# Differential attention of a two-block kernel: value product feature by feature in three fp32r passes, norm by a product with ones

## The chip, the cores and the metric

The program runs on one core of one Trainium2 chip. Its metric is the device time of one execution in microseconds, as a median over runs. Everything is float32 in and out, batch 1, 512 tokens, width 1024.

## The reference, cut to what matters

Two blocks follow each other. The first (pooling mixer, sparse attention, feed-forward) is not touched. The second has two layers; each projects the normed input, runs three branches (gated linear attention "a", sparse attention "b", differential attention "c"), gates them, merges them and adds the result. The change is in branch c of both layers:

```
def _diff(q, k, v, ..., lambda_init):          # 4 heads of 2 x 64, values of 128
    q, k = _rms(q, qn_g), _rms(k, kn_g)
    p = softmax(where(allowed, q k^T * 64**-0.5, -inf))      # two maps per head, 512 x 512
    attn = p[:, :, 0] - lam * p[:, :, 1]
    out = attn @ v                                           # [512 tokens, 4 heads, 128]
    out = out * rsqrt(mean(out**2, over 128) + 1e-6) * (1 - lambda_init)

y_c = _diff(...) * silu(cz)                     # then y_c @ w_br[2], gated and merged
```

`allowed` is causal by chunks of 64, so of the 4 x 4 blocks of 128 x 128 per map only the 10 on and below the diagonal are computed.

## The kernel before, in words

**Number format.** Most products are made of float32 operands split into a high part (rounded to fp32r, written "r" here) and a low part (the rest). A product is then three matmuls, high x high, low x high, high x low (helper `three`, L286 to L291, and `high_first`, L293 to L304, which puts the products with the low part of the weights last so that it can arrive late). A matmul on unsplit float32 tiles is one instruction that the profile shows as two records.

**Weights.** They come as a stream of chunks of 128 x 2048 through two slots. SyncE loads a chunk, ScalarE makes its high part (`act_conv`, L278), VectorE (`dve_conv`, L283) or GpSimd its low part. Every section of the layer ("cz", "cgate", "gv", "gq", "cbr" and so on) has a fixed order of tiles; TensorE puts a tile in one of two PSUM banks `pp` and waits, through the semaphore `evac`, until the tile two before has been copied out (`pe_tile`, L309). The sections "in the wide form" (`pe_wide`) have tokens on the partitions of the result; `pe_tile_part` gives features on the partitions.

**Order.** Each engine's program of a layer is written out by hand (`pe_layer`, `act_layer`, `dve_layer`, `pool_layer`, L1421 to L2160); engines meet at semaphores only, and each engine runs strictly in its order. Attention steps are laced between projection pieces, so that TensorE has matmuls while ScalarE and VectorE do the softmax.

**Branch c, a head.** In step s (0 to 4, each with quarters i = 0 to 3) TensorE computes head s's scores in the banks `ps` and `pt` (`pe_score_diff`, L1337), VectorE the row maxima, ScalarE the exponentials and their sums (`act_exp_diff`, L1353), VectorE combines the two maps (`dve_combine`, L1363): p1 = p1 + c * p2, unnormalised, with c = -lam * sum1 / sum2. It also keeps 1 / sum1 (`r1`, L1378). In step s+1 the blocks are turned by TensorE transposes (`pe_turn_attn`, L1243) and copied back by ScalarE over the attention tile (`act_turned_attn`, L1258). `pe_pv_tm` (L1265) then multiplies: the turned attention block is the stationary operand, 128 value columns move, in plain float32, 10 blocks per head; the output has tokens on partitions. VectorE scales it by r1 (`dve_o_diff`, L2087), GpSimd squares it and multiplies it by the gate `z_c` (L2139, L2141), VectorE sums the squares (`dve_o_sum`), ScalarE takes one square root for all, VectorE inverts it (`inverse_root`) and scales four tiles (L1997). In the middle of section "gq" TensorE turns these four tiles (16 transposes, L1209), ScalarE and VectorE split them into high and low parts (L1220, L1224), and section "cbr" multiplies them by the branch weights.

**Order on VectorE in a step s = 1 or 2**: at i = 2 the maxima of row block 3, `dve_combine` of row block 2, the low part of a turned key (L1224), the low part of a weight chunk (L283); at i = 3 `dve_combine` of row block 3. In step 3 there is no key to turn. TensorE multiplies the value blocks 2 and 3 of the head before at i = 0 of the step after that, ahead of the scores of its head.

**Order on ScalarE at the end**: a weight chunk, the sigmoid of the first half of the gates (`xT`, L1752), section "gq" tile 0 copied out, four high parts, "gq" tile 1 copied out (L1758), a weight chunk (L278), the sigmoid of the second half (`work`, L1763), two exponentials and a small one for branch a (L1766, L1767), then the tiles of "cbr" copied out (L1046).

Of the kernel before, what the change touches and what calls it, by code (L numbers as in the profile page):

```python
# [107 lines left out]
WIDE = ("gki", "bq", "bk", "bv", "cq", "ck", "cv", "cz", "gv", "gz")  # L108
KI = 344
KI_IK, KI_ALR, KI_IW = 256, 320, 336  # L110
FOUR_BANKS = ("q", "gki", "bq", "bk", "bv", "cz")
# [17 lines left out]
def two_block_kernel(nc, x_in, pos_in, w_in, vec_in, cst_in, msk_in, cmpw_in, small_in, out):  # L129
    with ExitStack() as ctx:  # L130
# [7 lines left out]
        xT = sb("xT", [P, KT, S], F32)  # L138
        hhi, hlo = sb("hhi", [P, KT, S], F32R), sb("hlo", [P, KT, S], F32R)
# [15 lines left out]
        alr_f = sb("alr_f", [P, S], F32)  # L155
        p_odd = sb("p_odd", [P, EVEN], F32)
# [62 lines left out]
        o_out, ring_in, v_in = sem("o_out"), sem("ring_in"), sem("v_in")  # L219
        cs_ready, cs_sub, cs_exp, cs_p = sem("cs_ready"), sem("cs_sub"), sem("cs_exp"), sem("cs_p")  # L220
# [26 lines left out]
        ix_acc, x_kept = sem("ix_acc"), sem("x_kept")  # L247
        o_turned, o_sq, o_sum, o_gated = sem("o_turned"), sem("o_sq"), sem("o_sum"), sem("o_gated")
# [446 lines left out]
        vr = [[rv(9216 + 1024 * b + 512 * y, 4, P) for y in range(2)] for b in range(2)]  # L695
        yr = [rv(0, 4, S), rv(2048, 4, S)]
# [16 lines left out]
        o_tm, osq_f = xT[:, 4:8, :], wv(14848, S)  # L713
# [5 lines left out]
        gq_f, kd_f, za_f, la_f = wv(6144, 2, S), wv(7168, 4, 256), wv(8192, 4, 256), wv(9216, 4, 256)  # L719
# [6 lines left out]
        r1 = [nst[:, 232 + 4 * b:236 + 4 * b] for b in range(2)]  # L726
# [17 lines left out]

        def turned_attn(s, kb):

            p = attn(s)[:, P * kb + STEP * kb:]
            return bass.AP(p.tensor, p.offset, [p.ap[0], [STEP, QT - kb], [1, P]])

        def low_no(v):  # L750

            l = (v - U1) // 8
            return 4 * (U1 + 4 * l + v - U1 - 8 * l)
# [489 lines left out]
        def pe_turn_attn(pe, l, v, s, kbs):  # L1243

            if kbs[0] == 0:
# [2127 lines left out]
```

## Time and profile before

| | us |
|---|---|
| median of 3 runs (1859.45 to 1859.85) | 1859.71 |
| the profiled execution's own time | 1859.72 |
| its span, first to last instruction | 1857.8 |
| TensorE matmuls busy | 1853.4 |
| weight loads of TensorE | 1537.6 |
| VectorE | 1239.6 |
| ScalarE | 899.4 |
| GpSimd | 397.6 |

The granted TensorE clock is 1.000 over the whole span, that is 2.4 GHz. A busy time is the union of the instructions' durations; matmuls are pipelined, so the distance from one start to the next (the start column of the timeline) is what a matmul costs, and its duration is longer.

### The profile page before, as it was taken

How to read it: one execution, taken by the hardware profiler on the slowest of the kernel's cores; microseconds unless marked ns; L12 is line 12 of the kernel's file. 1: busy time of each engine (PE TensorE's matmuls, PEld its weight loads, DVE VectorE, ACT ScalarE, POOL GpSimd, SP SyncE). 2: the span in 40 equal slices, each digit the busy share in tenths (PEclk: the TensorE clock that was granted, in tenths of full speed). 3: DMA queues.
4: the chain of work that ended last, by engine and by line, in shares of the span. 5: the costliest groups of instructions: out<-in, count | busy, mean ns of one | idle time of the engine just before them, and what ended most of it. 6: DMA issues, size and time to landing. Idle time of an engine off the chain costs nothing.

```text
span 1857.8 us, 25108 instructions
## 1 busy us (share of the span) xinstructions
PE 1853.4 (100%) x9597; PEld 1537.6 (83%) x9597; DVE 1239.6 (67%) x2022; ACT 899.4 (48%) x1417; POOL 397.6 (21%) x211
## 2 busy tenths in 40 slices
PE   9999999999999999999999999999999999999999
PEld 7977778788898988788888888888888888888887
DVE  7888657684783876688656755465689665666553
ACT  6564565544443455534455554444543445646442
POOL 1020012240440530245010000131235101010211
PEclk9999999999999999999999999999999999999999
DMA  6211113222232243222122123224122222112321
GB/s 243 97 69 69 46 68 139 94 99 100 91 114 91 91 145 127 91 91 91 69 91 94 46 91 114 108 97 159 69 91 91 79 81 91 71 69 91 137 91 68
DMA packets 26894, 178.98 MB, mean 96 GB/s; under 512 B 3232, under 2 KB 4128, under 8 KB 6560
## 3 DMA queue, kind: packets, MB, share of 16 engines
q1 hardware_dynamic: 24768, 163.97, 24.4%
q10 hardware_dynamic: 2016, 13.51, 1.9%
q8 instruction: 73, 1.20, 0.3%
q14 instruction: 37, 0.30, 0.0%
HBM read 171.18 MB, written 6.29 MB: 96 GB/s over the span
## 4 chain that ended last, share of the span: by engine, by line
PE 99%; DVE 0%; DMA 0%; ACT 0%; DVEq 0%; issue 0%; ACTq 0%
PE pp L299 34%; PE pp L303 17%; PE pp L289 9%; PE pp L291 9%; PE pp L290 9%; PE po L299 4%; PE po L303 2%; PE po L979 1%; PE po L1269 1%; PE pt L950 1%; PE po L291 1%; PE po L290 1%; PE po L289 1%; PE ps L1347 1%; PE po L1209 1%; PE ps L856 1%
## 5 line engine op out<-in xcount | busy, mean ns | idle before, releaser
L283 DVE TENSOR_TENSOR wlo<-wraw,whi 128x2048 fp32r<-128x2048 f32 x116 | 271.4, 2340 | 186.6 <-ACT whi L278 186.0
L278 ACT ACTIVATE whi<-wraw 128x2048 fp32r<-128x2048 f32 x143 | 273.2, 1910 | 63.3 <-PE pp L303 63.3
L299 PE MATMUL pp<-hhi,whi 128*128 128x512 f32 x639 | 259.0, 405 | 0.0
L299 PE MATMUL pp<-hlo,whi 128*128 128x512 f32 x639 | 249.7, 391 | 0.0
L299 PE MATMUL pp<-whi,hhi 128*128 128x512 f32 (+2 forms) x528 | 206.3, 393 | 0.0
L299 PE MATMUL pp<-whi,hlo 128*128 128x512 f32 (+2 forms) x528 | 199.9, 380 | 0.0
L303 PE MATMUL pp<-hhi,wlo 128*128 128x512 f32 x639 | 173.9, 390 | 0.0
L2114 POOL TENSOR_TENSOR wlo<-wraw,whi 128x2048 fp32r<-128x2048 f32 x26 | 120.4, 4632 | 248.7 <-ACT whi L278 248.7
L289 PE MATMUL pp<-split,whi 128*128 128x512 f32 x402 | 156.8, 390 | 0.0
L291 PE MATMUL pp<-split,wlo 128*128 128x512 f32 x402 | 156.4, 389 | 0.0
L290 PE MATMUL pp<-split,whi 128*128 128x512 f32 x402 | 156.4, 389 | 0.0
L299 PEld LDWEIGHTS pp<-hhi,whi 128*128 128x128 f32 x639 | 120.0, 188 | 33.8 <-issue 8.9
L303 PE MATMUL pp<-wlo,hhi 128*128 128x512 f32 (+2 forms) x528 | 144.0, 380 | 0.0
L303 PEld LDWEIGHTS pp<-hhi,wlo 128*128 128x128 f32 x639 | 119.9, 188 | 25.8
L299 PEld LDWEIGHTS pp<-hlo,whi 128*128 128x128 f32 x639 | 120.2, 188 | 22.3 <-issue 0.5
L289 PE MATMUL pp<-hhi,whi 128*128 128x512 f32 x303 | 118.9, 392 | 0.0
L291 PE MATMUL pp<-hhi,wlo 128*128 128x512 f32 x303 | 117.9, 389 | 0.0
L290 PE MATMUL pp<-hlo,whi 128*128 128x512 f32 x303 | 117.9, 389 | 0.0
L299 PEld LDWEIGHTS pp<-whi,hhi 128*128 128x128 f32 x528 | 99.3, 188 | 17.7 <-issue 1.9
L303 PEld LDWEIGHTS pp<-wlo,hhi 128*128 128x128 f32 x528 | 97.0, 188 | 18.8
L299 PEld LDWEIGHTS pp<-whi,hlo 128*128 128x128 f32 x528 | 99.4, 188 | 15.4
L299 PE MATMUL pp<-split,whi 128*128 128x512 f32 x444 | 107.2, 390 | 0.0
(544 smaller groups left out, 3703.9 us busy)
## 6 DMA issues: line engine op xcount, KB each, us to landing
wraw<-weights SPq DMA_DIRECT2D x150, 1024.0 KB, 4.8
out_t<-xT ACTq DMA_DIRECT2D x4, 1024.0 KB, 4.1
xT<-out_t ACTq DMA_DIRECT2D x2, 2048.0 KB, 8.8
work<-cmp_w ACTq DMA_DIRECT2D x1, 2048.0 KB, 8.7
xT<-x_t ACTq DMA_DIRECT2D x1, 2048.0 KB, 7.5
wraw<-weights SPq DMA_DIRECT2D x7, 256.0 KB, 7.8
xT<-x_t SPq DMA_DIRECT2D x3, 512.0 KB, 8.4
out_t<-xT SPq DMA_DIRECT2D x3, 512.0 KB, 2.6
```

Source lines behind the costliest of these rows:

```text
L278: nc.scalar.activation(whi[:, slot, :], wraw[:, slot, :], ACT.Copy).then_inc(w_hi, 1)
L283: nc.vector.tensor_tensor(wlo[:, slot, :], wraw[:, slot, :], whi[:, slot, :].bitcast(F32), ALU.subtract).then_inc(w_lo, 1)
L289: nc.tensor.matmul(out_ap, ah, bh, start=start, stop=False)
L290: nc.tensor.matmul(out_ap, ah, bl, start=False, stop=False)
L291: return nc.tensor.matmul(out_ap, al, bh, start=False, stop=stop)
L299: nc.tensor.matmul(out_ap, *pair, start=(start and n == 0 and part == 0), stop=False)
L303: last = nc.tensor.matmul(out_ap, *pair, start=False, stop=(stop and n == len(steps) - 1))
L856: last = nc.tensor.matmul(front_bank(s, i, g)[:, at:at + w], qr[t % 2][x][rows, i * P:i * P + P], kr[b][y][rows, 0:w], start=(x + y == 0 a ...
L950: last = nc.tensor.transpose(pt[g][:, at:at + P], p_buf(s, g)[:, STEP * i + kb * P:STEP * i + kb * P + P], ident)
L979: last = nc.tensor.matmul(po[g][y_rows(g), kb * P:S].rearrange("p (i m) -> p i m", m=P), v32[:, kb, at:at + 64], turned(s, g, kb), start=( ...
L1209: last = nc.tensor.transpose(bank[:, i * P:i * P + P], src[:, i * P:i * P + P], ident)
L2114: nc.gpsimd.tensor_tensor(wlo[:, c % 2, :], wraw[:, c % 2, :], whi[:, c % 2, :].bitcast(F32), ALU.subtract).then_inc(w_lo, 1)
```

## The change

It replaces, in both layers:

- section "cz" (the gate) from the wide form to `pe_tile_part`, features on partitions; weights are laid out accordingly; it no longer uses the banks `po`
- `pe_pv_tm` by `pe_pv_diff`: the values, split by GpSimd into two parts, are stationary; the turned attention moves, 512, 384, 256 and 128 columns wide, in three passes; ScalarE's copy of the turned blocks rounds to fp32r, and VectorE makes their low part (`dve_turned_attn`); the waits of `pe_turn_attn`, `pe_score_diff` and the value product are on VectorE's `pt_lo` instead of ScalarE's `pt_hi`
- `dve_combine`: both maps are normalised there (one more pass over the row block), `r1` goes
- the result of the value product is squared and copied out by ScalarE (`act_o_diff`); GpSimd multiplies, squares and makes the low part of the square; TensorE sums squares over the features with a matrix of ones, two passes per head, in section "gv"; ScalarE takes the inverse root of a full 128 x 512 tile per head; VectorE corrects it (`dve_o_norm`); no transposes follow
- on ScalarE, the sigmoid of `xT` moves from before section "gq" to behind it

```
-WIDE = (..., "cv", "cz", "gv", "gz")
+WIDE = (..., "cv", "gv", "gz")
-FOUR_BANKS = ("q", "gki", "bq", "bk", "bv", "cz")
+FOUR_BANKS = ("q", "gki", "bq", "bk", "bv")

 def pe_turn_attn(...):
-                pe.wait_ge(pt_hi, 4 * v)
+                pe.wait_ge(pt_lo, 4 * v)
...
-                pe.wait_ge(pt_hi, 4 * v + kbs[0] - 1)
+                pe.wait_ge(pt_lo, 4 * v + kbs[0] - 1)
-        def pe_pv_tm(pe, v, s, kb, bank):
-            pe.wait_ge(pt_hi, 4 * v + kb + 1)
-            for i in range(kb, QT):
-                last = nc.tensor.matmul(bank[:, i * P:i * P + P], attn(s)[:, STEP * i + kb * P:STEP * i + kb * P + P],
-                                        c_f[:, kb, s * P:s * P + P], start=(kb == 0 and i == 0), stop=(kb == QT - 1))
+        def dve_turned_attn(dve, v, s, kbs):
+            for kb in kbs:
+                dve.wait_ge(pt_hi, 4 * v + kbs[-1] + 1)
+                nc.vector.tensor_tensor(turned_low(s, kb), turn_bank(kbs, kb).rearrange("p (i m) -> p i m", m=P),
+                                        turned_attn(s, kb).bitcast(F32), ALU.subtract).then_inc(pt_lo, 1)
+        def pe_pv_diff(pe, l, v, s, kb, bank):
+            if kb == 0:
+                pe.wait_ge(diff_v, 4 * l + s + 1)
+            pe.wait_ge(pt_lo, 4 * v + kb + 1)
+            last = three(bank[:, kb * P:S].rearrange("p (i m) -> p i m", m=P), [y[:, kb, :] for y in diff_parts[s % 2]],
+                         (turned_attn(s, kb), turned_low(s, kb)), kb == 0, kb == QT - 1)
 def pe_score_diff(...):
             if i == 2 and s >= 2:
-                pe.wait_ge(pt_hi, 4 * (U1 + 8 * l + 4 + s - 1))
+                pe.wait_ge(pt_lo, 4 * (U1 + 8 * l + 4 + s - 1))
 def dve_combine(...):
-            nc.vector.reciprocal(c[:, 0:1], sums[:, 2 * i + 1:2 * i + 2])
+            nc.vector.reciprocal(c, psum_[s % 2][:, 2 * i:2 * i + 2])
             dve.drain()
-            nc.vector.scalar_tensor_tensor(out=c[:, 1:2], in0=c[:, 0:1], scalar=nlam[:, l:l + 1],
-                                           in1=sums[:, 2 * i:2 * i + 1], op0=ALU.mult, op1=ALU.mult)
+            nc.vector.tensor_scalar(c[:, 1:2], c[:, 1:2], nlam[:, l:l + 1], None, ALU.mult)
+            nc.vector.tensor_scalar(p1, p1, c[:, 0:1], None, ALU.mult)
...
-                nc.vector.reciprocal(r1[s % 2], sums.rearrange("p (i g) -> p i g", g=2)[:, :, 0])
 def pe_layer(pe, l):
...
             for p in range(4, 8):
                 pe_wide(pe, "gv", l, p)
-            pe_tile_part(pe, "gq", l, 0, 0, 1)
-            for x in range(4):
-                pe.wait_ge(y_scaled, 8 * l + x + 1)
-                pe_t(pe, D_BANKS[x], o_tm[:, x, :])
-            pe_tile_part(pe, "gq", l, 1, 0, 1)
+                for x in {4: range(3), 5: range(3, 4)}.get(p, ()):
+                    pe.wait_ge(o_turned, 4 * l + (3 if x < 3 else 4))
+                    pe.wait_ge(o_sq, 8 * l + x + 1)
+                    nc.tensor.matmul(norm_banks[x][:, :], ones_r[:, :], square_hi[x], start=True, stop=False)
+                    nc.tensor.matmul(norm_banks[x][:, :], ones_r[:, :], square_lo[:, x, :], start=False, stop=True).then_inc(t_done, 1)
+            for n in range(2):
+                pe_tile_part(pe, "gq", l, n, 0, 1)
 ScalarE:
+        def act_o_diff(act, l, s):
+            act.wait_ge(pv_done, U1 + 8 * l + 4 + s + 1)
+            nc.scalar.activation(square_hi[s], po[s % 2][:, :], ACT.Square)
+            nc.scalar.activation(o_fm[:, s, :], po[s % 2][:, :], ACT.Copy).then_inc(o_turned, 1)
 def act_layer(act, l):
...
+            for x in range(4):
+                act.wait_ge(t_done, tb + 8 + x + 1)
+                nc.scalar.activation(o_fm[:, x, :], norm_banks[x][:, :], ACT.Abs_reciprocal_sqrt, scale=1.0 / P,
+                                     bias=con(C_EPS)).then_inc(o_root, 1)
...
-            nc.scalar.activation(xT[:, 0:4, :], xT[:, 0:4, :], ACT.Sigmoid)
+            for x in range(4):
+                act.wait_ge(o_norm, 4 * l + x + 1)
+                nc.scalar.activation(yr[0][:, x, :], z_c[:, x, :], ACT.Copy, scale=con(C_1ML + l)).then_inc(t_hi, 1)
...
             act_next(act, "gq", l, c0, slot0)
+            nc.scalar.activation(xT[:, 0:4, :], xT[:, 0:4, :], ACT.Sigmoid)
             nc.scalar.activation(wv(4096, 4 * S), wv(4096, 4 * S), ACT.Sigmoid).then_inc(gates_in, 1)
 VectorE:
+        def dve_o_norm(dve, l, x):
+            y, t, z = o_fm[:, x, :], norm_t[x % 2], z_c[:, x, :]
+            dve.wait_ge(o_root, 4 * l + x + 1)
+            nc.vector.scalar_tensor_tensor(out=t, in0=y, scalar=-0.5 / P, in1=y, op0=ALU.mult, op1=ALU.mult)
+            nc.vector.scalar_tensor_tensor(out=t, in0=norm_banks[x][:, :], scalar=EPS * P, in1=t, op0=ALU.add, op1=ALU.mult)
+            dve.wait_ge(o_gated, 8 * l + x + 1)
+            nc.vector.scalar_tensor_tensor(out=z, in0=t, scalar=1.5, in1=z, op0=ALU.add, op1=ALU.mult).then_inc(o_norm, 1)
 GpSimd:
+            def diff_values_in(s):
+                if s >= 2:
+                    pool.wait_ge(pv_done, v0 + 4 + s - 1)
+                split_pool(pool, diff_parts[s % 2], c_f[:, :, s * P:s * P + P]).then_inc(diff_v, 1)
...
+                nc.gpsimd.tensor_tensor(z, z, o, ALU.mult)
+                nc.gpsimd.tensor_tensor(o, o, o, ALU.mult)
+                nc.gpsimd.tensor_tensor(square_lo[:, s, :], o, square_hi[s].bitcast(F32), ALU.subtract).then_inc(o_sq, 1)
```

## Rows read from the trace of the kernel before

**Rows 1.** The page: busy times, and the chain that ended last

```profile
PE 1853.4 (100%) x9597; PEld 1537.6 (83%) x9597; DVE 1239.6 (67%) x2022; ACT 899.4 (48%) x1417; POOL 397.6 (21%) x211
...
PE 99%; DVE 0%; DMA 0%; ACT 0%; DVEq 0%; issue 0%; ACTq 0%
```

**Rows 2.** Timeline of TensorE, branch c: start, duration, what, count

```profile
1032.85 1.05 PE L1269 MATMUL po<-work 128*128 128x128 f32 x8
1033.74 0.49 PE L1254 MATMUL pt<-cst,work 128*128 128x128 f32 x3
...
1039.62 0.83 PE L1269 MATMUL po<-work 128*128 128x128 f32 x6
...
1074.56 0.83 PE L1269 MATMUL po<-work 128*128 128x128 f32 x6
```

**Rows 3.** Timeline of TensorE, value products of branch b in three passes

```profile
899.01 0.33 PE L289 MATMUL po<-split 128*128 128x384 f32 x1
...
899.53 0.38 PE L1233 MATMUL pt<-cst,work 128*128 128x128 f32 x2
...
903.61 0.28 PE L289 MATMUL po<-split 128*128 128x256 f32 x1
...
903.96 0.27 PE L1233 MATMUL pt<-cst,work 128*128 128x128 f32 x1
...
907.22 0.28 PE L290 MATMUL po<-split 128*128 128x128 f32 x1
907.34 0.27 PE L291 MATMUL po<-split 128*128 128x128 f32 x1
```

**Rows 4.** Timeline of TensorE, section "cbr", product of 512 columns

```profile
1121.16 0.39 PE L289 MATMUL pp<-split,whi 128*128 128x512 f32 x1
...
1121.84 0.39 PE L289 MATMUL pp<-split,whi 128*128 128x512 f32 x1
```

**Rows 5.** Timeline of TensorE, the turns within section "gq"

```profile
1106.43 1.03 PE L1209 MATMUL po<-cst,xT 128*128 128x128 f32 x8
...
1108.09 0.48 PE L299 MATMUL pp<-hhi,whi 128*128 128x512 f32 x1
```

**Rows 6.** Timeline of VectorE, branch c, steps 1 and 3

```profile
1035.43 0.75 DVE L1224 SCALAR_TENSOR_TENSOR split<-po,vec,split 128x512 fp32r<-128x512 f32 x1 [1.28 <-ACT split L1220]
1036.10 2.28 DVE L283 TENSOR_TENSOR wlo<-wraw,whi 128x2048 fp32r<-128x2048 f32 x1
...
1039.49 0.17 DVE L1378 RECIPROCAL nst<-nst 128x4 f32<-128x4 f32 x1
...
1072.80 0.17 DVE L1378 RECIPROCAL nst<-nst 128x4 f32<-128x4 f32 x1
```

**Rows 7.** Timeline of ScalarE, branch c, step 1

```profile
1038.44 0.55 ACT L1262 ACTIVATE work<-pt 128x256 f32<-128x256 f32 x2 [3.04 <-PE pt L1254]
```

**Rows 8.** Groups by form, VectorE: count, then busy us, mean ns, idle

```profile
L1388 DVE TENSOR_SCALAR work<-work,stat 128x512 f32<-128x512 f32 x8 | 3.9, 486 | 0.6
...
L1000 DVE TENSOR_TENSOR split<-pt,split 128x256 fp32r<-128x256 f32 x8 | 3.4, 424 | 10.1 <-ACT split L994 10.1
```

**Rows 9.** Timeline of ScalarE, sections "gq" and "cbr"

```profile
1106.69 1.92 ACT L1752 ACTIVATE xT<-xT 128x2048 f32<-128x2048 f32 x1
...
1113.84 0.60 ACT L1758 ACTIVATE work<-pp 128x512 f32<-128x512 f32 x1 [2.45 <-PE pp L303]
...
1118.07 1.28 ACT L1766 ACT_TABLE_LOAD   x1
...
1120.63 0.60 ACT L1046 ACTIVATE work<-pp 128x512 f32<-128x512 f32 x1
```

**Rows 10.** Timeline of GpSimd, branch c, step 2

```profile
1045.97 1.28 POOL L2141 TENSOR_TENSOR xT<-xT,work 128x512 f32<-128x512 f32 x1
```

**Rows 11.** Timeline of VectorE, the same moment

```profile
1046.10 1.30 DVE L1374 SCALAR_TENSOR_TENSOR work<-work,nst 128x128 f32<-128x128 f32 x1
...
1047.84 0.48 DVE L1374 SCALAR_TENSOR_TENSOR work<-work,nst 128x256 f32<-128x256 f32 x1
```

More of the change, by code:

```diff
@@ L695, in two_block_kernel @@
         vr = [[rv(9216 + 1024 * b + 512 * y, 4, P) for y in range(2)] for b in range(2)]
+        diff_low = [rv(TRI * b, TRI) for b in range(2)]
+        diff_parts = [[rv(2560 + 1024 * b + 512 * y, 4, P) for y in range(2)] for b in range(2)]
         yr = [rv(0, 4, S), rv(2048, 4, S)]
@@ L712, in two_block_kernel @@
         z_b, cq_tm, ck_tm, z_c = xT[:, 0:4, :], xT[:, 4:8, :], wv(4096, 4, S), wv(6144, 4, S)
-        o_tm, osq_f = xT[:, 4:8, :], wv(14848, S)
+        o_fm = xT[:, 4:8, :]
+        square_hi = [rv(4608, S), rv(9984, S), rv(10496, S), work_r[:, 14848:15360]]
+        square_lo = xT_r[:, 4:8, :]
+        norm_banks = (po[0], ps[0], ps[1], po[1])
+        norm_t = [split_f[:, 7168 + 512 * b:7680 + 512 * b] for b in range(2)]
         p2_f = [wv(14592, P), wv(13568, 256), wv(14080, 384), wv(13568, S)]
@@ L1485, in pe_layer @@
             pe.wait_ge(y_ready, 4 * l + 4)
-            for p in range(6):
-                pe_wide(pe, "cz", l, p)
+            for n in range(3):
+                pe_tile_part(pe, "cz", l, n, 0, 1)
             tb, v0 = tb + 8, v0 + 4
@@ L1492, in pe_layer @@
             pe_t(pe, ps[1], ck_tm[:, 0, :])
-            for p in range(6, 8):
-                pe_wide(pe, "cz", l, p)
+            pe_tile_part(pe, "cz", l, 3, 0, 1)
             for s in range(4 + 1):
@@ L1507, in pe_layer @@
                     for kb in diff_values(s, i) if s >= 1 and i > 0 else ():
[L1508 to L1509 removed]
                         if kb == 0 and s == 4:
                             pe.wait_ge(o_turned, 4 * l + 2)
[L1512 removed]
+                        pe_pv_diff(pe, l, v0 + s - 1, s - 1, kb, po[(s - 1) % 2])
                     if s >= 1 and diff_turns(s, i):
@@ L1693, in act_layer, with gate_tile @@
                 sq_c(4 + tt), ck_tm[:, tt, :], ACT.Square).then_inc(ln_sq, 1))
-            act.wait_ge(ln_sum, 4 * l + 2)
+            act.wait_ge(ln_sum, 3 * l + 2)
             nc.scalar.activation(ln_root, ln_ss, ACT.Sqrt, scale=1.0 / 64, bias=con(C_EPS)).then_inc(ln_rt, 1)
-            act_after_first(act, "cz", l)
-            for i in range(2):
-                act_wide(act, "cz", l, i, z_c[:, i, :], ACT.Silu)
+            cz, _, tz, _ = section("cz", l)
+            pz, sz = par_of("cz", l)
+            def gate_tile(n):
+                act.wait_ge(mm_done, tz + n + 1)
+                nc.scalar.activation(z_c[:, n, :], pp[(pz + n) % 2][:, :], ACT.Silu).then_inc(evac, 1)
+            for n in range(2):
+                gate_tile(n)
+            act_next(act, "cz", l, cz, sz)
             tb, v0 = tb + 8, v0 + 4
@@ L1702, in act_layer @@
             act_t(act, tb + 1, kr[0][0], ps[1], col(V_CK + l))
-            for i in range(2, 4):
-                act_wide(act, "cz", l, i, z_c[:, i, :], ACT.Silu)
+            for n in range(2, 4):
+                gate_tile(n)
             act.dma_start(wa2_f[:, :], small_in[:, 6 * P + 256 * l:6 * P + 256 * l + 256]).then_inc(wa2_in, 16)
@@ L1712, in act_layer @@
                             act.wait_ge(tr_done, 4 * (v0 + s - 2) + 4)
+                        if i == 0 and s >= 2:
+                            act_o_diff(act, l, s - 2)
                         for rows in by_bank(diff_rows(s, i)):
@@ L1858, in dve_layer @@
             par0, _ = par_of("iq", l)
+            if l == 0:
+                nc.vector.tensor_copy(ones_r[:, :], ones)
             c0 = section("gki", l)[0]
@@ L2012, in dve_layer, with y_low @@
                                            op1=ALU.subtract).then_inc(la_split, 1)
+            def y_low(x):
+                dve.wait_ge(t_hi, tb + 8 + x + 1)
+                nc.vector.scalar_tensor_tensor(out=yr[1][:, x, :], in0=z_c[:, x, :], scalar=con(C_1ML + l),
+                                               in1=yr[0][:, x, :].bitcast(F32), op0=ALU.mult,
+                                               op1=ALU.subtract).then_inc(t_lo, 1)
+            y_low(0)
             dve_conv(dve, c0 + 3, (slot0 + 1) % 2)
-            for x in range(4):
-                dve_t(dve, tb + 8 + x, [y[:, x, :] for y in yr], D_BANKS[x], con(C_1ML + l))
+            for x in range(1, 4):
+                y_low(x)
             dve_next(dve, "gq", l)
             dve.wait_ge(decayed, l + 1)
+            dve.drain()
             for i in range(QT):
@@ L3260, in _stream @@
         columns(br[1], 512)
-        rows(w[:, 5720:6232])
+        columns(w[:, 5720:6232])
         columns(gate[:, 2048:3072])
```

111 lines of the change are left out of this document (50 added, 61 removed).

## The prediction

> **What bounds the kernel now.** Three views, in this order. First the busy times and the chain that ended last: TensorE is busy in 1853.4 of 1857.8 us and the chain is 99% TensorE [rows 1]. So the time is the sum of what TensorE issues plus whatever it waits for; work saved on VectorE, ScalarE or GpSimd is worth nothing unless TensorE would have waited for it, and work added there costs nothing until it makes TensorE wait. Second the timeline of TensorE through branch c, to price matmuls by the distance between starts, since durations overlap. Third the timelines of the other engines at the places where TensorE meets a semaphore, to see how long before TensorE's arrival each is fulfilled. I found no wait of TensorE in branch c in either layer; layer 1 repeats layer 0, so all sums are per layer and then doubled. They are made against the profiled execution's own 1859.72 us (span 1857.8), which is 0.01 from the median.
>
> **A. What TensorE issues.** The value product before: an instruction of 128 moving columns is two records, and eight records take 1032.85 to 1033.74, 0.11 us a record [rows 2]. Per head 20 records: 2.22 us. After: three passes over 512, 384, 256 and 128 columns. 512 columns: 0.68 for three (1121.16 to 1121.84) [rows 4]. 384: 0.52, 256: 0.35, and 128: 0.12 a pass, so 0.35 [rows 3]; a pass of 128 columns costs no less than one of 256. Sum 1.90, so 0.32 saved per head and 1.3 per layer. Little, because the narrow blocks pay three passes for what two records did.
>
> The turns behind: 16 transposes take 1106.43 to 1108.09, 1.66 us [rows 5]; in their place 8 products with ones over 512 columns, 8 x 0.227 = 1.81 [rows 4]. About +0.1. Section "cz" has 96 matmuls of 512 columns in either form: nothing. Its four banks become two, so tile 2 needs tile 0 copied out, but a tile lasts 24 x 0.227 = 5.4 us and the copy 0.6; that work hides it. The transposes of the attention blocks stay. A = -1.2 per layer, between -0.8 and -1.6.
>
> **B. The wait for the low parts.** TensorE takes blocks 2 and 3 of head 0 at 1039.62 [rows 2]. Before, it needed ScalarE's copies alone, done at 1038.44 + 0.55 = 1038.99 [rows 7]: 0.6 to spare. Now it needs VectorE's subtraction, which stands in VectorE's order behind the low part of a key, the low part of a weight chunk (2.28) and the combination of row block 3. That chain is set by ScalarE's copy of the turned key (the wait shown at 1035.43) and runs without a pause to 1039.49, where the combination is over [rows 6]. So VectorE can't begin before about 1039.5, even if nothing were added. Added: the normalising pass over 512 columns, 0.49 less its overlap with the small instruction ahead of it, and r1 gone: +0.3. Then the subtraction of 256 columns, 0.42 [rows 8]. The key's turn itself comes 0.2 earlier, as block 0's product is 0.2 shorter. Ready: 1039.49 - 0.2 + 0.3 + 0.42 + 0.05 for the signal = 1040.1. TensorE arrives 0.35 earlier than before (blocks 0 and 1), at 1039.3. It waits 0.8. Block 3 (0.3 later) is ready in time, as block 2 takes 0.35.
>
> For head 1 the same pattern stands 17.88 us on. All of it hangs on events of TensorE in the same step, so the wait comes back rather than being absorbed by the first. ScalarE has there two more passes over a PSUM bank (square and copy) ahead of the exponentials, GpSimd five operations instead of two; I add 0.2: 1.0. For head 2 (TensorE at 1074.56 [rows 2]) VectorE is done at 1072.80 [rows 6], early, because no key is turned in that step. But block 1's subtraction now stands ahead of the chunk: +0.6 (nearest row: 0.42 for 256 columns [rows 8]), the two longer combinations +0.6, and its own wait for ScalarE's copy of block 1 some 0.3; then 0.42 for block 2. 1072.80 + 0.6 + 0.6 + 0.3 + 0.42 = 1074.7 against 1074.2: 0.4 to 0.5, taken as 0.4. Head 3 has the blocks one by one with 1.4 us of other matmuls between a turn and its product: nothing.
>
> B = 0.8 + 1.0 + 0.4 = 2.2 per layer. From below: if the passes overlap better and head 2 makes it, 1.0. From above: one GpSimd operation of 1.28 in the way in each of three steps, 2.2 + 2.3 = 4.5.
>
> Why such an operation can be in the way: a VectorE pass over 128 columns that began at 1046.10, while GpSimd's operation of 1045.97 to 1047.25 ran, took 1.30, against 0.48 for 256 columns just after it [rows 10, 11]. By the Trainium skill ("SBUF — State Buffer", section "SBUF: two separate sides") VectorE, when it reads two SBUF inputs, and GpSimd share one port pair as an exclusive lock held for the whole instruction. The trace agrees: the pass ended just after GpSimd's did. It speaks against this change, which gives GpSimd more; it is the rival "lock" below.
>
> **C. The sigmoid that moved.** ScalarE's order in the tail decides when "cbr" tile 0 is copied out, and TensorE needs this before tile 2, as `pp` has two banks. Before: copied at 1120.63 + 0.60 = 1121.23 [rows 9]; TensorE began tile 2 at 1121.84 [rows 4]. 0.6 to spare. ScalarE went from "gq" tile 1 at 1113.84, which TensorE sets, without a pause to that copy. The sigmoid of `xT` stood before all this at 1106.69, followed by a stretch in which ScalarE waited 2.45 for TensorE [rows 9]: it was free. Now it stands inside the chain: 1.92. Its table load comes with it, since the logarithm's table is in use until then: 1.28, as the one at 1118.07 [rows 9]. The copy comes at 1124.4, TensorE waits 3.2 - 0.6 = 2.6. Nothing else on TensorE lies between to soak it up: the distance from the end of "gq" to "cbr" tile 2 is unchanged. C = 2.6 per layer. From below 0, if the load or the order differ from what I read; from above 3.2, if the spare 0.6 is taken by something else.
>
> By the Trainium skill ("ScalarE: Activation LUTs", "What ACT_TABLE_LOAD costs") a switch costs about 2.66 us with its drain. The rows at 1118.07 show 1.28 and the next instruction directly behind; with the page's figure C would be 4.0, an estimate from that page, and the total 2.8 higher. I go by the row.
>
> **D. The tail of the norm.** Inverse root of four full tiles on ScalarE (4 x 0.6 and a load of 1.28), four GpSimd products, twelve VectorE passes of about 0.7 instead of four. From TensorE's last product with ones to "cbr" there are two pieces of "gv" and two tiles of "gq", 24 + 48 matmuls of 0.227, 16 us, and 2.7 more for branch a's products. VectorE's new chain, laid out in order: norm 8.5, chunk 2.3, the wait for the logarithm, branch a's 4.7, the first low part 0.7, chunk 2.3, three low parts 2.0; it ends about 1.5 to 3 before TensorE needs each. D = 0, above 2 per layer with the lock.
>
> **Sum.** A + B + C + D = -1.2 + 2.2 + 2.6 + 0 = +3.6 per layer, +7.2 for two: 1866.9.
>
> **Rivals.** About 0.2%, 3.7 us, is what a measurement of this kernel can tell from no change.
>
> 1. One of the two waits does not come. Without B: -2.4 + 5.2 = +2.8, 1862.5. Without C: -2.4 + 4.4 = +2.0, 1861.7. For: B is a difference of 0.8 between chains 5 us long, and C rests on one table load and 0.6 us of slack. Against: both chains run without a pause in the rows. Chance 0.21.
>
> 2. Not slower: TensorE's arithmetic alone decides, since both waits are hidden. Place: the value product; price -1.2 per layer; 1859.7 - 2.4 = 1857.3. It decides if VectorE's low parts are ready by 1039.3 and the copy of "cbr" tile 0 by 1121.8. For: before the change TensorE never waited in this stretch. Against: rows 6, where VectorE is busy past 1039.3 even without the additions. Chance 0.08; it is within 0.2%, as 2.4 is below 3.7.
>
> 3. The lock: GpSimd's extra operations (about 3.5 us more per head, and four products beside VectorE's norm) hold VectorE up. A delay of 1.28 in two of three steps and 1 in D: +3.6 per layer above some of my B, say +2 per layer net. 1866.9 + 4 = 1870.9. For: rows 10 and 11. Against: at the critical ends of the steps GpSimd has long finished; its work falls where VectorE has slack, and subtractions that read PSUM take only one SBUF input. Chance 0.18.
>
> **How the numbers follow.** Forecast 0.53, rival 1 0.21, rival 2 0.08, rival 3 0.18. The forecast's own range is 1863.5 to 1869.5 from the bounds of A and B. The whole: from rival 1's 1861.5 to 1872, which leaves out rival 2, some of rival 1's tail and the worst of the lock. Slower by over 0.2% (above 1863.4): forecast, lock and a little of rival 1, 0.71. Within 0.2%: most of rival 1 and of rival 2, 0.25. Faster: 0.04.
>
> **What would show it.** Value products on "po" in three passes, 1.9 us a head, and no plain float32 matmul there: A. TensorE idle before the 256-column product in three steps of a layer, released by VectorE's subtraction: B; if it is released by GpSimd (values) or ScalarE, B has the wrong cause. TensorE idle of 2 to 3 us inside "cbr" before its third tile, released by ScalarE's copy, with the sigmoid of `xT` and a table load right before: C. If the table load stays ahead of "gq", C is 1.3. TensorE idle before "cbr" tile 0 would mean D. VectorE passes of over 1 us for 128 to 512 columns at those places mean the lock. The forecast is wrong if TensorE shows no idle time in branch c.

## The result, and the profile after the change

The changed kernel takes 1869.99 us (median of 6 executions, 1868.11 to 1870.25), the kernel before it 1859.76 in the same comparison (1859.45 to 1860.46): ratio 1.0052, 95% interval 1.0041 to 1.0062. That is 10.2 us slower; forecast were 7.1 more (1866.9, whole range 1861.5 to 1872.0; the forecast's own range ended at 1869.5). The profiled execution took 1870.24 with a span of 1868.5, and all working below is made against it. The six times fall into two groups, four from 1869.9 to 1870.25 with a mean granted clock of 0.999 and two near 1868.15 with 1.000; experiment 5 says what lies between them.

The page of the changed kernel, busy times and the chain that ended last (beside [rows 1]):

```profile
PE 1855.7 (99%) x9517; PEld 1533.2 (82%) x9517; DVE 1264.6 (68%) x2071; ACT 912.4 (49%) x1439; POOL 443.9 (24%) x243
...
PE 95%; ACT 1%; DVE 1%; DVEq 1%; DMA 0%; issue 0%; ACTq 0%; SPq 0%
```

TensorE issues 80 matmuls fewer and is no longer 99% of the chain: VectorE and ScalarE have entered it. Who they are stands in the waits of TensorE (what waited and on whom: total us, times, longest):

```profile
PE po L294 <- DVE split L1286: 4.1, 6, 1.1
PE pp L294 <- ACT work L1059: 4.1, 2, 2.2
PE pt L2375 <- DVE work L2866: 1.2, 1, 1.2
```

The third row is in the kernel before as well, outside the layers. The first is the value product waiting for VectorE's low part, three times per layer; the second is "cbr" waiting for ScalarE's copy, once per layer. Both are new. To see why the first comes, VectorE in step 1 of layer 0 (start, duration, what), which answers to [rows 6]:

```profile
1035.64 0.75 DVE L1237 SCALAR_TENSOR_TENSOR split<-po,vec,split 128x512 fp32r<-128x512 f32 x1
1036.31 2.28 DVE L288 TENSOR_TENSOR wlo<-wraw,whi 128x2048 fp32r<-128x2048 f32 x1
1038.51 0.16 DVE L1393 RECIPROCAL nst<-nst 128x2 f32<-128x2 f32 x1
1038.75 0.21 DVE L1395 TENSOR_SCALAR nst<-nst,stat 128x1 f32<-128x1 f32 x1
1038.88 0.48 DVE L1396 TENSOR_SCALAR work<-work,nst 128x512 f32<-128x512 f32 x1
1039.43 0.75 DVE L1398 SCALAR_TENSOR_TENSOR work<-work,nst 128x512 f32<-128x512 f32 x1
1040.10 0.62 DVE L1286 TENSOR_TENSOR split<-pt,work_r 128x256 fp32r<-128x256 f32 x2
```

and TensorE at the same moment, beside its product at 1039.62 in [rows 2]:

```profile
1040.67 0.36 PE L294 MATMUL po<-work_r,split 128*128 128x256 f32 x1 [0.80 <-DVE split L1286]
1040.86 0.28 PE L295 MATMUL po<-split 128*128 128x256 f32 x1
```

VectorE runs without a pause from the low part of the key to the subtraction, which begins at 1040.10; TensorE could have begun 0.80 us earlier than it did. For the second wait, ScalarE from the copy of "gq" tile 1 to that of "cbr" tile 0, beside [rows 9]:

```profile
1115.60 0.60 ACT L1791 ACTIVATE work<-pp 128x512 f32<-128x512 f32 x1 [2.88 <-PE pp L308]
1116.09 1.91 ACT L283 ACTIVATE whi<-wraw 128x2048 fp32r<-128x2048 f32 x1
1118.02 1.28 ACT L1793 ACT_TABLE_LOAD   x1
1119.31 1.92 ACT L1793 ACTIVATE xT<-xT 128x2048 f32<-128x2048 f32 x1
1121.13 1.90 ACT L1794 ACTIVATE work<-work 128x2048 f32<-128x2048 f32 x1
1123.05 1.28 ACT L1797 ACT_TABLE_LOAD   x1
1124.35 1.09 ACT L1797 ACTIVATE work<-pt 128x512 f32<-128x512 f32 x2
1125.32 0.19 ACT L1798 ACTIVATE work<-po 128x16 f32<-128x16 f32 x1
1125.61 1.09 ACT L1059 ACTIVATE work<-pp 128x512 f32<-128x512 f32 x2
```

and TensorE there. Matmuls before the wait start 0.23 us apart, as in [rows 4]; behind it, 0.43 apart for a while:

```profile
1123.43 0.39 PE L295 MATMUL pp<-split,whi 128*128 128x512 f32 x1
1123.66 0.39 PE L296 MATMUL pp<-split,wlo 128*128 128x512 f32 x1
1126.26 0.75 PE L294 MATMUL pp<-split,whi 128*128 128x512 f32 x1 [2.22 <-ACT work L1059]
1126.81 0.63 PE L295 MATMUL pp<-split,whi 128*128 128x512 f32 x1
1127.24 0.63 PE L296 MATMUL pp<-split,wlo 128*128 128x512 f32 x1
```

Two windows of equal length side by side (length, busy time of the engines, then the granted clock as the third number from the end):

```profile
1126.34:1129.76 3.42, 3.42 (x8) 2.69 (x9) 3.27 (x7) 0.36 (x1) 0.00 (x0) 0.50 0.00 0
1129.76:1133.18 3.42, 3.42 (x16) 2.80 (x15) 1.67 (x3) 0.60 (x1) 0.00 (x0) 1.00 0.00 0
```

8 matmuls where 16 fit: for 3.42 us the granted clock was half of full speed (1.2 instead of 2.4 GHz), so half of 3.42, 1.7 us, is lost.

Laying the starts of TensorE's matmuls in the two traces side by side, and taking the waits from start to start (so with the overlap of two matmuls, 0.17 us, that a wait takes away), the difference of 10.7 us between the spans of the two profiled executions comes out so:

| part | forecast, both layers | layer 0 | layer 1 | sum |
|---|---|---|---|---|
| A, TensorE's own instructions | -2.4 | -0.96 | -1.01 | -1.97 |
| B, waits for low parts of blocks 2 and 3 | +4.4 | 0.97 + 0.97 + 0.47 | 1.32 + 0.97 + 0.47 | +5.17 |
| C, wait for the copy of "cbr" tile 0 | +5.2 | 2.38 | 2.02 | +4.40 |
| D, tail of the norm | 0 | 0.29 | 0.65 | +0.94 |
| half clock behind C | not forecast | 1.7 | 0 | +1.7 |
| start of the program, before the change | not forecast | | | +0.42 |

The sum is 10.66. Row A is the remainder; it includes 0.11 us per layer that the first matmul behind C's wait loses, so up to that point it is -1.07 and -1.12. C and D belong together: D is spent just ahead of C's wait and shortens it, and C + D is 2.67 in both layers. The last row is no part of the change: within the first 15 us of the program the profiles of this case drift apart by up to 0.9 us (against the kernel before, -0.27 in experiment 2 and +0.64 in experiment 4).

### The profile page after: what moved, and what is told of

Its sections match the earlier page's. It is cut to its first block, busy times and chain, and to the rows that moved or that the text cites. A ratio compares the mean times of both kernels' runs of the same rounds, so it can differ in the third digit from the quotient of the medians.

```text
span 1868.5 us, 25085 instructions
## 1 busy us (share of the span) xinstructions
PE 1855.7 (99%) x9517; PEld 1533.2 (82%) x9517; DVE 1264.6 (68%) x2071; ACT 912.4 (49%) x1439; POOL 443.9 (24%) x243
## 4 chain that ended last, share of the span: by engine, by line
PE 95%; ACT 1%; DVE 1%; DVEq 1%; DMA 0%; issue 0%; ACTq 0%; SPq 0%
PE pp L304 33%; PE pp L308 16%; PE pp L294 9%; PE pp L296 9%; PE pp L295 9%; PE po L304 3%; PE po L308 2%; PE po L294 1%; PE po L296 1%; PE po L295 1%; PE po L992 1%; PE pt L963 1%; PE ps L1372 1%; PE ps L869 1%; DVEq L1394 1%; PE ps L295 1%
## 5 line engine op out<-in xcount | busy, mean ns | idle before, releaser
L304 PE MATMUL pp<-hhi,whi 128*128 128x512 f32 x703 | 283.9, 404 | 0.0
L304 PE MATMUL pp<-hlo,whi 128*128 128x512 f32 x703 | 274.7, 391 | 0.0
L304 PE MATMUL pp<-whi,hhi 128*128 128x512 f32 (+2 forms) x496 | 193.6, 392 | 0.0
L308 PE MATMUL pp<-hhi,wlo 128*128 128x512 f32 x703 | 189.8, 390 | 0.0
L304 PE MATMUL pp<-whi,hlo 128*128 128x512 f32 (+2 forms) x496 | 187.4, 380 | 0.0
L304 PEld LDWEIGHTS pp<-hhi,whi 128*128 128x128 f32 x703 | 132.0, 188 | 36.3 <-issue 8.9
L308 PEld LDWEIGHTS pp<-hhi,wlo 128*128 128x128 f32 x703 | 131.9, 188 | 28.5
L304 PEld LDWEIGHTS pp<-hlo,whi 128*128 128x128 f32 x703 | 132.3, 188 | 24.8 <-issue 0.5
L308 PE MATMUL pp<-wlo,hhi 128*128 128x512 f32 (+2 forms) x496 | 135.4, 379 | 0.0
L294 PE MATMUL pp<-hhi,whi 128*128 128x512 f32 x303 | 118.9, 392 | 0.0
L296 PE MATMUL pp<-hhi,wlo 128*128 128x512 f32 x303 | 117.9, 389 | 0.0
L295 PE MATMUL pp<-hlo,whi 128*128 128x512 f32 x303 | 117.9, 389 | 0.0
L1028 POOL CAST split<-work 128x512 fp32r<-128x512 f32 x22 | 14.6, 666 | 383.4 <-PE po L296 204.6
```

The source lines that it names most:

```text
L294: nc.tensor.matmul(out_ap, ah, bh, start=start, stop=False)
L295: nc.tensor.matmul(out_ap, ah, bl, start=False, stop=False)
L296: return nc.tensor.matmul(out_ap, al, bh, start=False, stop=stop)
L304: nc.tensor.matmul(out_ap, *pair, start=(start and n == 0 and part == 0), stop=False)
L308: last = nc.tensor.matmul(out_ap, *pair, start=False, stop=(stop and n == len(steps) - 1))
```

## Experiments

My theory: four terms as in the forecast, B set by VectorE's queue (the chunk's low part ahead of the passes), C by ScalarE's order, the half clock by TensorE's standing still, D by VectorE and GpSimd holding each other up. The kernels are the changed kernel with one thing altered, unless said otherwise; the kernel before, beside them, took 1859.85 to 1859.98 (1859.76 beside the changed kernel), so a difference between two experiments is known to about 0.2 us.

**1. The sigmoid back where it was** (e1_sigmoid_back).

```
+            nc.scalar.activation(xT[:, 0:4, :], xT[:, 0:4, :], ACT.Sigmoid)   # ahead of y's high parts
...
-            nc.scalar.activation(xT[:, 0:4, :], xT[:, 0:4, :], ACT.Sigmoid)   # behind the copies of "gq"
```

> The changed kernel with the sigmoid of xT put back ahead of the high parts of y, where it stood before the change. My theory: TensorE's idle time of 2.2 and 1.9 us within cbr (waiting for ScalarE's copy of tile 0) goes in both layers, and with it the stretch of 3.4 us at half clock behind the first of them. 1870.0 - 4.4 - 1.7 = 1863.9 us. The high parts of y come 3.2 us later but VectorE does not reach their low parts before 1114.7, so nothing is added. Rival: the copy is late for another reason (the low parts of y, GpSimd's lock on VectorE's passes); then most of the idle time stays and the time is above 1868.

Measured 1864.01 (1863.67 to 1864.1), ratio 1.0022 [1.0012, 1.0031], clock 1.00 in all 11 executions. Of the new waits this one is left:

```profile
PE po L294 <- DVE split L1286: 4.1, 6, 1.1
```

The wait at "cbr" is gone, and 5.98 us with it, for the 4.40 of C and the 1.7 of the half clock, 6.1. C is shown, cause and size.

**2. The chunk's low part moved behind the value product** (e2_chunk_after): in steps 1 to 3 VectorE makes the low part of the "cgate" chunk at the end of quarter 3 instead of quarter 2.

```
-                    if 1 <= s <= 3 and i == 2 or s == 4 and i == 0:
+                    if 1 <= s <= 3 and i == 3 or s == 4 and i == 0:
```

> The changed kernel with VectorE's low part of the weight chunk of cgate moved, in steps 1 to 3, from the end of quarter 2 to the end of quarter 3, behind the combination of row block 3 and the low parts of turned blocks 2 and 3. My theory: the wait of TensorE for these low parts (0.97, 0.97 and 0.47 us a layer, start to start) comes from the place in VectorE's queue; the low parts are then ready at about 1039.7 against 1039.5, so 4.8 of 5.2 us go: 1865.2 us. Rival: the added passes alone or GpSimd's operations make them late; then the wait stays above half a us in each step and the time above 1867.

Measured 1867.77 (1866.67 to 1868.73), ratio 1.004 [1.0026, 1.0054]: a miss, half of the gain. Its waits of TensorE:

```profile
PE pp L294 <- ACT work L1059: 4.0, 2, 2.2
...
PE pp L308 <- DVE wlo L288: 0.9, 2, 0.5
PE pt L1267 <- issue: 0.5, 2, 0.2
```

The row of the value products is gone, so the chunk's place is a cause of B (the added pass is the other, experiment 6). But 2.29 us of VectorE's time don't vanish: the low part of the "gv" chunk is late now (0.65 per layer from start to start), and two turns (0.30 and 0.40), as I read it since the maxima and with them the exponentials are late; the row of the turns names no releaser. 1.35 of the 2.41 in layer 0 are given back.

**3. The sigmoid in ScalarE's gap** (e3_sigmoid_gap): between the copies of "gq" tile 0 and tile 1, where ScalarE waits for TensorE anyway.

```
                 nc.scalar.activation(gq_f[:, n, :], pp[(par0 + n) % 2][:, :], ACT.Copy, scale=0.125).then_inc(evac, 1)
+                if n == 0:
+                    nc.scalar.activation(xT[:, 0:4, :], xT[:, 0:4, :], ACT.Sigmoid)
...
-            nc.scalar.activation(xT[:, 0:4, :], xT[:, 0:4, :], ACT.Sigmoid)   # behind the copies of "gq"
```

> The changed kernel with the sigmoid of xT between the copies of gq tile 0 and gq tile 1, where ScalarE waits 2.9 us for TensorE. My theory: 3.2 us of sigmoid and table load nearly fit there, gq tile 1 is copied 0.25 us later, and the copy of cbr tile 0 is in time: as e1, 1863.9 us (up to 0.4 more). Rival: as for e1, above 1868.

Measured 1863.78 (1863.57 to 1864.15), ratio 1.0021 [1.0012, 1.003]. As experiment 1: it is not the sigmoid that costs, but its standing between a copy that TensorE sets and one that TensorE waits for.

**4. Both** (e4_both: 2 and 3 together).

> e2 and e3 together. My theory: both waits and the half-clock stretch go, which leaves the 1.0 us a layer that TensorE's own instructions save, less 0.3 to 0.7 us a layer of waiting for the low parts of y: 1870.0 - 5.0 - 4.3 - 1.7 = 1859.0 us, 0.8 below the kernel before. Rival: one of the two was shadowed by the other (a gain that the other wait takes back); then the sum of e2's and e3's gains is not reached, 1861 or more.

Measured 1861.57 (1860.89 to 1862.07), ratio 1.0008 [0.9999, 1.0017]. A miss by 2.6, for the reason of experiment 2; the two gains (2.22 and 6.21) add up to the 8.42 measured. B and C are independent.

**5. TensorE kept at work during the wait** (e5_filler).

```
+            for _ in range(9):
+                nc.tensor.matmul(ps[0][:, :], ones_r[:, :], hhi[:, 0, :], start=True, stop=True)   # ahead of "cbr" tile 2
```

> The changed kernel, with nine 512-column products into a bank that nobody reads, just ahead of the product of cbr that waits for ScalarE's copy in both layers: 9 x 0.227 us = 2.04 us of work inside a wait of 2.2 to 2.4 us. Nothing else changes. Theory: the stretch of granted clock 0.50 (3.4 us long, 8 products at 0.427 instead of 0.227 us, so 1.7 us lost) follows TensorE's standing still; with TensorE at work it goes, the end of the wait itself stays where it was: the slower executions of the changed kernel (near 1870.0) are gone and all lie near 1868.2, the granted clock of the run is 1.00. Rival: the stretch comes whatever TensorE does ahead of it: 1869.9 as before, in some of the executions, and a stretch at 0.50 stays in the profile behind the wait.

Measured 1868.8 (1868.19 to 1869.38), ratio 1.0047 [1.0034, 1.006], granted clock 1.00 in all five. TensorE around the wait:

```profile
1123.40 2.22 PE L1577 MATMUL ps<-hhi,ones_r 128*128 128x512 f32 x9
1125.79 0.47 PE L294 MATMUL pp<-split,whi 128*128 128x512 f32 x1 [0.17 <-ACT work L1059]
1126.10 0.40 PE L295 MATMUL pp<-split,whi 128*128 128x512 f32 x1
```

The product still comes when ScalarE's copy lets it, but the ones behind it run at 0.23 us each: the half clock belongs to the idle time, and is what lay between the two groups of the changed kernel's times. (The median is 0.6 us above the 1868.2 expected. Start to start, the nine products delay the one behind them by 0.1 in layer 1; the rest is not explained.) In the profiles of this case no idle stretch of TensorE inside the layers of up to 1.15 us was followed by half a clock, one of two of 1.85 and 1.86 us was, and 8 of the 10 from 2.17 to 2.69 us. The half clock began between 0.4 us before and 1.3 us after the end of the wait. What decides between two equal waits no run here shows.

**6. Without the normalising pass** (e7_no_pass_gap: experiment 3, and the pass left out; the attention's values are not normalised).

```
-            nc.vector.tensor_scalar(p1, p1, c[:, 0:1], None, ALU.mult)
```

> The kernel with the sigmoid of xT between the two copies of gq (1863.8, no wait at cbr), and with VectorE's normalising pass over the turned block left out in all steps (part of the work: the values of the attention are then not normalised). What is left of the cost per layer is the three waits of the value products for VectorE's low parts (2.41 us from start to start). Theory: a wait is late by what stands in VectorE's queue between the last exponentials and the low part, the conversion of the cgate chunk (0.75 us) and the two passes over the block; without the normalising pass each wait is shorter by that pass alone, 0.35 us in the two 256-column steps and 0.3 to 0.47 us in the last: 1.1 us per layer, so 1861.6, and each of the first two waits stays at about 0.6 us. Rival: the added passes themselves are the whole cost and the chunk's place in the queue is harmless: the waits fall to nothing, 1859.0.

Measured 1860.86 (1860.38 to 1863.11), ratio 1.0006 [0.9997, 1.0014], 2.9 below experiment 3.

```profile
PE po L294 <- DVE split L1286: 1.6, 4, 0.4
```

The first two waits of each layer fell to 0.40, the third went: the theory, with 1.19 in layer 0 instead of 1.1 and 1.54 in layer 1, where the first wait had been 0.35 longer (and layer 1's D fell by 0.35). The added pass is about half of B, the queue in front of it the rest. The rival, which had the waits fall to nothing, is out.

**7. The chunks on GpSimd** (e9_pool_chunk: experiment 3, and three low parts of chunks per layer made by GpSimd).

```
-                    if 1 <= s <= 3 and i == 2 or s == 4 and i == 0:
+                    if s == 4 and i == 0:
+                        dve.wait_ge(w_lo, section("cgate", l)[0] + s + 1)
...
+            pool.wait_ge(w_lo, c0 + 2)
+            low_part(c0 + 2)
             for s in range(4):
...
+                if s < 2:
+                    low_part(c0 + s + 3)
```

> The kernel with the sigmoid of xT between the two copies of gq (1863.8), and with the low parts of three chunks of cgate (and the first of gv) made by GpSimd instead of VectorE, in the steps in which VectorE also makes the low parts of the turned blocks. Moving them to the end of the step on VectorE gave back 1.35 of 2.41 us per layer, as the product of the gv chunk and a turn came to wait. Theory: off VectorE nothing new stands in the way: all three waits go (2.41 us per layer, 4.8 in all), 1859.0, of which the arithmetic saved is -1.0 per layer and the waits for the low parts of y +0.3 to +0.7 are what is left: level with the kernel before or faster by up to 0.8 us. Rival: GpSimd takes the port that it shares with VectorE for some 2 us for each chunk, and VectorE's passes over the turned blocks run at its pace or wait behind it: half of the waits stay or new ones come, 1861 to 1864.

Measured 1874.24 (1869.62 to 1877.02), ratio 1.0074 [1.0062, 1.0086]: the rival, and worse than it said. GpSimd, then VectorE, in step 2:

```profile
1047.60 4.63 POOL L2153 TENSOR_TENSOR wlo<-wraw,whi 128x2048 fp32r<-128x2048 f32 x1
```

```profile
1048.07 4.32 DVE L1396 TENSOR_SCALAR work<-work,nst 128x256 f32<-128x256 f32 x1
1052.46 0.48 DVE L1398 SCALAR_TENSOR_TENSOR work<-work,nst 128x256 f32<-128x256 f32 x1
```

GpSimd needs 4.63 us for what takes VectorE 2.29, and a VectorE pass of 256 columns begun meanwhile ends 0.16 after it: 4.32 us, for 0.34 where GpSimd is idle. TensorE then waits 2.24 and 2.69 us, and the clock halves behind three of the four waits. By the Trainium skill ("SBUF — State Buffer", "SBUF: two separate sides") the port pair is locked for the whole instruction of the one that holds it; the trace agrees. The page names two kinds of VectorE passes that take the pair, those with two SBUF inputs and those in a mode of two ports; this one reads a single tensor, so by the page it is of the second kind. A pass is thus not safe for reading one SBUF tensor only. Rival 3's "against" spoke of subtractions that read PSUM, and for these it holds: in the changed kernel a pass of the norm that reads a bank (L2131, shown in experiment 8) begins four times with about 1.07 us of a GpSimd operation left and takes its usual 0.69, and L1286 twice takes its usual 0.56 for 384 columns with 0.36 to 0.39 left.

**8. The same, with GpSimd's gate products cut to one column** (e8_pool_less; most of `o_gated` is not gated).

```
-                nc.gpsimd.tensor_tensor(z_c[:, x, :], z_c[:, x, :], o_fm[:, x, :], ALU.mult).then_inc(o_gated, 1)
+                nc.gpsimd.tensor_tensor(z_c[:, x, 0:1], z_c[:, x, 0:1], o_fm[:, x, 0:1], ALU.mult).then_inc(o_gated, 1)
```

> The last kernel (chunks' low parts on GpSimd), with GpSimd's products of the gate cut to one column (work left out: o_gated is not gated but in one column). Asks where the 0.3 to 0.7 us per layer come from by which the products of cbr wait for VectorE's low parts of y at the end of a layer. Theory: GpSimd's four products there (1.3 to 1.75 us each) and VectorE's (1.77 us instead of 0.69 for the same form alone) hold each other up; without them VectorE's operations take 0.69 us, the low parts come in time, and 0.3 to 0.7 us per layer go: 1.0 us below the run before it, 1858.0. Rival: the wait is VectorE's own queue (reciprocal root, two products and low part for each block): VectorE's operations may shrink but TensorE still waits 0.3 us or more in each layer, less than 0.3 us gained in all.

Measured 1873.3 (1870.77 to 1874.92), ratio 1.0071 [1.0058, 1.0084]; beside half clocks that come and go behind the long waits this time says little, the trace more. In the changed kernel, GpSimd's gate products lie beside VectorE's norm (GpSimd, VectorE, then TensorE's eight products of "cbr" tile 0):

```profile
1096.63 6.41 POOL L2197 TENSOR_TENSOR work<-work,xT 128x512 f32<-128x512 f32 x4
```

```profile
1098.41 1.77 DVE L2135 SCALAR_TENSOR_TENSOR work<-split_f,work 128x512 f32<-128x512 f32 x1 [0.41 <-POOL work L2197]
1100.11 1.78 DVE L2129 SCALAR_TENSOR_TENSOR split_f<-xT 128x512 f32<-128x512 f32 x1
1101.96 0.69 DVE L2131 SCALAR_TENSOR_TENSOR split_f<-ps,split_f 128x512 f32<-128x512 f32 x1
```

```profile
1118.13 2.28 PE L304 MATMUL pp<-split,whi 128*128 128x512 f32 x8
```

Without them, VectorE and TensorE:

```profile
1102.29 0.69 DVE L2137 SCALAR_TENSOR_TENSOR work<-split_f,work 128x512 f32<-128x512 f32 x1
1102.90 0.68 DVE L2131 SCALAR_TENSOR_TENSOR split_f<-xT 128x512 f32<-128x512 f32 x1
```

```profile
1122.30 2.00 PE L304 MATMUL pp<-split,whi 128*128 128x512 f32 x8
```

VectorE's operations fall from 1.77 to 0.69, and TensorE's eight products from 2.12 and 2.47 us (start of the first to start of the next instruction) to 1.84 in both layers. From the norm's first pass to the first low part of y VectorE takes 16.38 us, and took 18.82 in layer 0 and 19.18 in layer 1: the 0.36 between the layers is that between their D. So D comes of GpSimd's products beside the norm, nearly all by the lock: the stretched passes of layer 0 lost 2.3 us, which VectorE's lead did not quite cover, and about 0.4 more is VectorE waiting for the first product itself, as its [0.41 <-POOL] shows.

**9. The chunk's low part in halves** (e10_half_chunk: experiment 3, and 1024 columns at the end of quarter 2, 1024 at the end of quarter 3; the new helper `dve_half`, not shown, does one half).

```
-                    if 1 <= s <= 3 and i == 2 or s == 4 and i == 0:
+                    if 1 <= s <= 3 and i >= 2:
+                        dve_half(dve, section("cgate", l)[0] + s + 1, (section("cgate", l)[0] + s + 1) % 2, i - 2)
+                    if s == 4 and i == 0:
```

> The kernel with the sigmoid of xT between the two copies of gq (1863.8), with VectorE's low part of the cgate chunk cut in two halves of 1024 columns in steps 1 to 3: one where it was (end of quarter 2), one at the end of quarter 3. Theory: the waits of the value products (0.97, 0.97 and 0.47 us from start to start per layer) come from the 2.29 us that the chunk takes ahead of the passes over the turned block; half of it (1.2 us) later they go, and what the whole chunk cost when moved to quarter 3 (0.30 and 0.40 us at the turns, 0.65 us at the gv chunk per layer) stays under the half: -2.4 per layer, 1859.0 +- 0.5. Rival: moving VectorE's work within the step only moves the wait, half of it gives half: about 0.5 us per layer come back at the turns and the gv chunk, or stay at the value products, 1860 to 1861.6.

Measured 1859.22 (1858.7 to 1859.54, 11 executions), ratio 0.9996 [0.9987, 1.0005]. VectorE, then TensorE, in step 1:

```profile
1036.00 1.22 DVE L295 TENSOR_TENSOR wlo<-wraw,whi 128x1024 fp32r<-128x1024 f32 x1
...
1038.78 0.62 DVE L1295 TENSOR_TENSOR split<-pt,work_r 128x256 fp32r<-128x256 f32 x2
1039.32 1.22 DVE L295 TENSOR_TENSOR wlo<-wraw,whi 128x1024 fp32r<-128x1024 f32 x1
```

```profile
1039.39 0.32 PE L303 MATMUL po<-work_r,split 128*128 128x256 f32 x1
```

1.1 us less stands ahead of the low part than in the changed kernel, and no value product waits; of what the whole chunk had cost later, 0.13 us of idle time at a turn is left per layer (0.3 from start to start), and 0.06 at the "gv" chunk in layer 1. That is the theory of B as a queue, in its size too.

**10. And y's low parts ahead of the weight chunk** (e11_half_low: experiment 9, and the order of five instructions in the tail).

```
-            y_low(0)
-            dve_conv(dve, c0 + 3, (slot0 + 1) % 2)
-            for x in range(1, 4):
+            for x in range(4):
                 y_low(x)
+            dve_conv(dve, c0 + 3, (slot0 + 1) % 2)
```

> The last kernel, and in the tail all four low parts of y made by VectorE before the low part of the weight chunk (2.29 us) that stood between the first and the other three. Theory: TensorE's eight products of cbr tile 0 then take 1.83 us instead of 2.12 and 2.47 (-0.29 and -0.65), and the chunk, 2.0 us later, still comes before its product: 0.9 us below the run before it, 1858.1, and so faster than the kernel before the change. Rival: the product of that chunk waits for its low part by more than this gives: 1859 to 1861.

Measured 1858.57 (1858.02 to 1859.23, 11 executions), ratio 0.9993 [0.9984, 1.0002]. TensorE's eight products take 1.84 us in both layers with the gate products in place, so D can also be bought off by order. All 11 times lie below all 21 of the kernel before (1859.36 to 1860.39), by 1.28 in the median; the interval of the ratio still takes in 1, so it is a small gain or none.

## Why the prediction was right, and what it missed

**The time** lies in the whole range, but 0.5 us above the forecast's own range of 1863.5 to 1869.5, and nearer to rival 3's 1870.9 than to the 1866.9: by the number alone the lock would have won. It is luck that the time lies there, as the 1.7 us that bring it there are the half clock, which the prediction did not price (experiment 5), and the waits came where and from whom A, B and C said. The range was also not what it said it was: the bounds of A and B give 1863.7 from below, and from above 1872.3 with B's 4.5, or 1867.7 with its 2.2; 1869.5 is neither.

**What bounds the kernel** held: every microsecond of the difference is TensorE's own work or a wait of it; 25 us more on VectorE, 13 on ScalarE and 46 on GpSimd cost nothing but at three places.

**A** came out at -0.98 per layer for -1.2, inside its bounds; without what is lost behind C's wait, -1.1. The products with ones against the turns gave +0.15 at their own places (forecast +0.1). The price of 0.35 for three 128-column passes was a little high (0.28 from start to start), so four heads should have saved 1.5, and saved 1.1. The traces show where the 0.4 is: behind each of the three waits the first product takes 0.19 to 0.23 us to the next start instead of 0.12, and behind the value products of heads 2 and 3 the next instruction starts 0.11 us after the last record, where before the change it was 0.03.

**B** was right in place, releaser and number of waits. Its first term was 0.80 of idle time as forecast, plus the 0.17 of overlap that a wait takes away, which the step did not count; the second 0.97 for 1.0, the third 0.47 for 0.4. In layer 1 the first wait was 1.32, as VectorE stood 0.43 us behind the reciprocal ahead of its passes, and 0.08 in layer 0; why, no row shows. The same pause stands in the profiles of experiments 1, 3 and 5, and not in those of 2, 6 and 9. "The wait comes back rather than being absorbed" held. Experiments 6, 9 and 2 show the cause.

**C** was right in place and cause. From the copy of "gq" tile 1 to that of "cbr" tile 0 ScalarE takes 10.01 us, and took 6.79 [rows 9]: 3.22 more for the 3.2 of the step. TensorE waits 2.38 and 2.02 for 2.6 since it has by then lost 0.29 and 0.65 to D. The load took 1.28 with the sigmoid directly behind it. By the Trainium skill ("ScalarE: Activation LUTs", "What ACT_TABLE_LOAD costs"), which counts about 2.66, 1.28 of load and 1.38 of drain, the wait would have been 4.0, an estimate from that page. The load agrees, the drain shows in no row, and the chain grew by 3.22, not 4.6: the measurement decides against the sum here.

**What failed is the step "C. The copy comes at 1124.4, TensorE waits"**, which priced a wait of TensorE at its own length. The wait of 2.2 us also brought 3.4 us at half the clock: +1.7 in four executions of six, to judge by the granted clock. This is half of the miss.

**D = 0** failed as a size: VectorE's chain "ends about 1.5 to 3 before TensorE needs each" was laid out with passes of 0.69, without GpSimd's four products that I had counted two lines above. Locked, it loses 2.3 us and TensorE waits 0.29 and 0.65. In the changed kernel this cost next to nothing, as C's wait stood behind it and grew shorter by it; without C it is a cost of its own (experiments 3 and 10). So rival 3 was partly true, in the tail alone; in the steps, where I had put most of it, the passes of 128 columns that it stretched (1.42 us, and 1.30 before the change) made TensorE wait nowhere. What is left of the miss is B's 0.8, A's 0.4, the program's start 0.4 and C and D's 0.1.

## What to carry to other kernels

When TensorE is the chain, price every operation put in front of a handover by the queue it joins: the pass of 0.48 and the sigmoid of 1.92 cost almost their full length, not since they are long but since the queue ahead ran without a pause. Cutting a large operation with slack (the 2.29 us chunk) in two halves around the urgent one removed three waits where moving it whole only moved them. Cost a TensorE wait of about 2 us at its length and, as a likely extra, half a clock behind it. Cost an elementwise VectorE pass with all its inputs in SBUF, if it begins beside a GpSimd operation, at what is left of GpSimd's time plus most of its own; one that reads PSUM was not held here.

## What the runs showed of the hardware

The granted clock fell to 0.50 for about 3.4 us around the end of a wait of TensorE, in 9 of 12 cases from 1.85 to 2.69 us, and in none of the five executions with nine matmuls in the wait. Kernels with such waits scatter by 2 to 7 us, the others by 0.4 to 1.2, but for two single executions 2 us off at a mean clock of 0.999 (one of experiment 6, one of the kernel before beside it), whose cause no profile shows. An elementwise VectorE pass of 128 columns or more, with all inputs in SBUF, that began inside a GpSimd operation was held until this ended and then took its own time less 0.1 to 0.2 us: 4.32 us for a pass of 0.34 (experiment 7), 1.77 for one of 0.69 (changed kernel). Not held were passes that read a PSUM bank (0.69 with 1.07 us of GpSimd's left), and VectorE's search for the eight largest of a row in SBUF (L1355, MAX8, 0.69 for 512 columns with 3.42 left). Once in the changed kernel it was the other way round: a GpSimd operation begun at 362.80, 0.16 us into a run of VectorE's SBUF passes that lasted until 369.74, took 9.20 us, and 2.40 is what the next of its size took. In three-pass form, a block of 128 columns costs 0.28 us, one of 256 0.35 and one of 512 0.68, against two plain records of 0.11 for each 128 columns: the narrowest block loses, the others gain.
